# Three fp32r passes for the spatial unit's token tiles 1 to 3, with the slab split when a layer begins

## The reference, cut to what matters

```
for l in range(DEPTH):                                   # 2 layers
    h = rms_norm(x, norm_mix_g[l])                       # 512 x 1024
    parts = jnp.split(h @ w_in[l], split_points, axis=-1)
    q, k_c, v_c, k_s, v_s, k_w, v_w, nsa_g, sgu_in, s5_in, branch_g = parts
    y_a = nsa_attention(..., sigmoid(nsa_g), ...) @ w_attn_o[l]
    y_b = spatial_gating(sgu_in, ...) @ w_sgu_o[l]       # sgu_in: 512 columns
    y_c = s5_layer(s5_in, a_re, a_im, log_step, ...) @ w_s5_o[l]
    x = x + (g_a * y_a + g_b * y_b + g_c * y_c) @ w_mix_o[l]
    x = x + hierarchical_moe(rms_norm(x, norm_ffn_g[l]), ...)
```

## Time and profile before

| | |
|---|---|
| median of three runs | 1870.75 us |
| the profiled execution, its own time | 1874.76 us |
| its span | 1873.1 us |
| PE busy | 1833.1 us (98%) |
| DVE busy | 988.0 us (53%) |
| ACT busy | 488.3 us (26%) |
| POOL busy | 152.4 us (8%) |
| mean granted TensorE clock | 0.995 |

### The profile page before, as it was taken

The page is one execution under the profiler, slowest core; times in us unless marked ns, Lnnn a source line. Parts: engine busy times, 40 slices in busy tenths (PEclk is TensorE's granted clock), DMA queues, the critical chain, the costliest instruction groups (busy, mean ns, idle before and its releaser), DMA issues. The chain is left out here.

```text
span 1873.1 us, 26669 instructions
## 1 busy us (share of the span) xinstructions
PE 1833.1 (98%) x10352; PEld 1149.9 (61%) x10353; DVE 988.0 (53%) x1926; ACT 488.3 (26%) x881; POOL 152.4 (8%) x241
## 2 busy tenths in 40 slices
PE   7999999999999999999999999999999999999996
PEld 3887777788445455454457977778874545455443
DVE  6874555667334343342479565557663334343444
ACT  5423444433111111101154244443321111111112
POOL 4700000050000000000055000000400000000000
PEclk9999999999999999999999999999999999999998
DMA  5232111344999999999732311113369999999995
GB/s 173 70 125 69 68 68 46 113 143 196 404 426 427 425 426 426 422 428 425 328 110 71 124 68 68 46 58 123 121 272 427 427 427 425 428 422 427 421 427 213
DMA packets 61296, 482.92 MB, mean 258 GB/s; under 512 B 10256, under 2 KB 23056, under 8 KB 31504
## 3 DMA queue, kind: packets, MB, share of 16 engines
q1 hardware_dynamic: 61200, 481.59, 63.6%
HBM read 476.59 MB, written 4.19 MB: 257 GB/s over the span
## 5 line engine op out<-in xcount | busy, mean ns | idle before, releaser
L1979 DVE TENSOR_TENSOR x_tokens<-x_tokens,ps 128x512 f32<-128x512 f32 x240 | 160.6, 687 | 223.3 <-PE ps L1116 221.9
L1131 PE MATMUL ps<-arena,branch 128*64 128x512 f32 x512 | 230.3, 603 | 4.7 <-DMA slabs<-in_expert_w_down 4.7
L1131 PE MATMUL ps<-slabs,branch 128*64 128x512 f32 x512 | 230.4, 603 | 0.0
L1140 PE MATMUL ps<-arena 128*64 128x512 f32 x512 | 225.0, 592 | 0.0
L1141 PE MATMUL ps<-arena 128*64 128x512 f32 x512 | 225.0, 592 | 0.0
L1140 PE MATMUL ps<-slabs,arena 128*64 128x512 f32 x512 | 224.9, 592 | 0.0
L1141 PE MATMUL ps<-slabs,arena 128*64 128x512 f32 x512 | 224.9, 592 | 0.0
L853 PE MATMUL ps<-h_hi,w_parts 128*128 128x512 f32 x768 | 210.8, 408 | 1.5 <-DVE w_parts L1586 1.5
L1140 PEld LDWEIGHTS ps<-slabs,arena 128*64 128x64 f32 x512 | 70.1, 137 | 146.4 <-issue 146.4
L1140 PEld LDWEIGHTS ps<-arena 128*64 128x64 f32 x512 | 70.0, 137 | 145.5 <-issue 145.2
L853 PEld LDWEIGHTS ps<-h_hi,w_parts 128*128 128x128 f32 x768 | 135.1, 188 | 38.8 <-issue 9.2
(11 more groups left out here) (368 smaller groups left out, 3074.4 us busy)
## 6 DMA issues: line engine op xcount, KB each, us to landing
arena<-in_expert_w_gate SPq DMA_DIRECT2D x32, 2048.0 KB, 12.2
arena<-in_expert_w_up SPq DMA_DIRECT2D x32, 2048.0 KB, 16.7
arena<-in_expert_w_down SPq DMA_DIRECT2D x32, 2048.0 KB, 9.6
slabs<-in_expert_w_down SPq DMA_DIRECT2D x32, 2048.0 KB, 14.1
slabs<-in_expert_w_gate SPq DMA_DIRECT2D x30, 2048.0 KB, 15.1
slabs<-in_expert_w_up SPq DMA_DIRECT2D x30, 2048.0 KB, 19.6
slabs<-in_gate_w SPq DMA_DIRECT2D x24, 1024.0 KB, 4.8
slabs<-in_dense SPq DMA_DIRECT2D x22, 1024.0 KB, 5.8
```

Of the source, the lines that this page charges most:

```text
L1131: done = nc.tensor.matmul(ps[64 * b:64 * b + 64, BANK_Y[half], :], hidT[:, k, CAP * b:CAP * (b + 1)], w_down[b][:, k, half * 512:(half + 1 ...
L1140: nc.tensor.matmul(ps[0:64, BANK_GU[b], :], xk, low[:, k, :], start=(k == 0), stop=(k == ND - 1), tile_position=(0, 0))
L1979: v.tensor_tensor(xs, xs, ps[:, banks[n % len(banks)], :], ALU.add).then_inc(s["back_added"], 1)
```

## The change

The spatial unit's tile 0 stays plain fp32. Tiles 1 to 3 are multiplied in three passes of fp32r. For this, slab 0 is split when the layer begins: its high parts go into the third slab place (where slab 2 used to be loaded), its low parts into the place `x_lo`/`xn_tokens`. ACT makes the high parts in two copies of 128x2048, DVE subtracts blocks 0 to 3 and POOL blocks 4 to 7. All four `nsa_job`s stand ahead of the three new jobs. `h_hi` and `h_lo` are made earlier and in the order 1, 2, 3, 0. Slab 2 is loaded once all four tiles are done, and its high copy on ACT stands behind the last spatial evacuation and the small gates' copy. The counts of the semaphores shift by the new increments (`SGU_HI`, `SGU_LO`).

```diff
+        sgu_hi = w_parts[:, 2 * SLAB:3 * SLAB].rearrange("p (k c) -> p k c", k=ND)
+        sgu_lo = x_lo_place[:, 0:SLAB].rearrange("p (k c) -> p k c", k=ND)
...
-                    free = {3: (s["proj_done"], J_S5), 4: ...
+                    free = {2: (s["proj_done"], J_S5), 3: (s["proj_done"], J_S5), 4: ...
...
+                    def parts_job(n, t):                                     # PE
+                        out = bank_p(n)
+                        at = slice(t * P, (t + 1) * P)
+                        for part, (h, w) in enumerate(((h_hi, sgu_hi), (h_lo, sgu_hi), (h_hi, sgu_lo))):
+                            if part < 2:
+                                pe.wait_ge(s[("h_hi_ready", "h_lo_ready")[part]], t)
+                            for k in range(ND):
+                                if t == 1 and part == 0 and k % 4 == 0:
+                                    pe.wait_ge(s["w_hi_ready"], k // 4 + 1)
+                                if t == 1 and part == 2:
+                                    pe.wait_ge(*((s["w_lo_ready"], k + 1) if k < 4 else (s["w_lo_pool"], k - 3)))
+                                last = nc.tensor.matmul(out, h[:, k, at], w[:, k, :], start=..., stop=...)
+                        last.then_inc(s["proj_done"], 1)
...
+                    token_job(J_SGU, w_sgu, 0, S, 0)
+                    pe.wait_ge(s["small_in"], 16)
                     for t in range(NT):
-                        token_job(J_SGU + t, w_sgu, 0, S, t)  (and nsa_job(t) behind tiles 1 to 3)
+                        pe.wait_ge(s["hT_ready"], max(t, 1))
+                        nsa_job(t)
+                    for t in range(1, NT):
+                        parts_job(J_SGU + t, t)
...
+                    if layer == 0: (the two rotary Sin activations, moved to the front)     # ACT
+                    act.wait_ge(slab_in[0], 16)
+                    for half in range(2):
+                        ks = slice(4 * half, 4 * half + 4)
+                        nc.scalar.activation(sgu_hi[:, ks, :], view(slab[0], ND, S)[:, ks, :], ACT.Identity).then_inc(s["w_hi_ready"], 1)
                     act.wait_ge(s["small_in"], 16)
-                    act.wait_ge(s["bparam_in"], 16)
                     nc.scalar.activation(s5_small[0], small["lstep"], ACT.Exp).then_inc(s["step_ready"], 1)
+                    token_hi(1)
+                    token_hi(2)
                     (Exp of the magnitude, Sin and cosine of the angle)
+                    token_hi(3)
+                    token_hi(0)
                     for t in range(NT):
                         evac(J_SGU + t, ...)
+                        if t == 0:
+                            split_hi(1)
                     nc.scalar.activation(nsa_parts, ps[:, BANK_S[0], :], ACT.Identity).then_inc(s["nsa_parted"], 1)
+                    split_hi(2)
...
+                    dve.wait_ge(s["w_hi_ready"], 1)                          # DVE, behind hT
+                    for k in range(4):
+                        v.tensor_tensor(sgu_lo[:, k, :], view(slab[0], ND, S)[:, k, :], sgu_hi[:, k, :], ALU.subtract).then_inc(s["w_lo_ready"], 1)
                     (step, angle chain)
+                    for t in range(1, NT):
+                        low_tokens(t)
                     (polar chain)
                     low_tokens(0)
-                    low_tokens(1)
                     split_lo(LO_PIECES)
-                    low_tokens(2)
                     (two products of powers)
-                    low_tokens(3)
                     split_lo(LO_PIECES)
...
+                    pool.wait_ge(s["w_hi_ready"], 2)                         # POOL, ahead of all else
+                    for k in range(4, ND):
+                        g.tensor_tensor(sgu_lo[:, k, :], view(slab[0], ND, S)[:, k, :], sgu_hi[:, k, :], ALU.subtract).then_inc(s["w_lo_pool"], 1)
```

More of the change, by code:

```diff
@@ L95 @@
 LO_PIECES = 4
+SGU_HI, SGU_LO = 2, 4
 LO_COLS = SLAB // 2 // LO_PIECES
@@ L715, in token_job @@
                         last.then_inc(s["proj_done"], 1)
+                    def parts_job(n, t):
[9 more added lines that the diff above has]
+                                    pe.wait_ge(*((s["w_lo_ready"], k + 1) if k < 4 else (s["w_lo_pool"], k - 3)))
+                                last = nc.tensor.matmul(out, h[:, k, at], w[:, k, :], start=(part == 0 and k == 0), stop=(part == 2 and k == ND - 1))
+                        last.then_inc(s["proj_done"], 1)
                     def value_job(t):
@@ L962, in _ @@
                         if n % 4 == 0:
-                            pe.wait_ge(s["w_hi_ready"], m + 1)
+                            pe.wait_ge(s["w_hi_ready"], SGU_HI + m + 1)
                         if n == 0:
@@ L1258, in _ @@
                     nc.scalar.activation(cos1, sincos[3], ACT.Sin).then_inc(s["polar_ready"], 1)
-                    if layer == 0:
-                        nc.scalar.activation(rope_sin, rr, ACT.Sin, scale=rot_sign).then_inc(s["pro_act"], 1)
-                        nc.scalar.activation(rope_cos, r2, ACT.Sin).then_inc(s["pro_act"], 1)
+                    token_hi(3)
+                    token_hi(0)
                     def split_hi(k):
@@ L1512, in _, with low_tokens @@
                         ins.then_inc(s["hT_ready"], 1)
+                    def low_tokens(t):
+                        dve.wait_ge(s["h_hi_ready"], t if t >= 1 else NT)
+                        dve.wait_ge(s["nsa_done"], t + 1)
+                        cols = slice(t * P, (t + 1) * P)
+                        v.tensor_tensor(h_lo[:, :, cols], tile_of(t), h_hi[:, :, cols], ALU.subtract).then_inc(s["h_lo_ready"], 1)
+                    if layer == 0:
+                        dve.wait_ge(s["pro_act"], 2)
+                    dve.wait_ge(s["w_hi_ready"], 1)
+                    for k in range(4):
+                        v.tensor_tensor(sgu_lo[:, k, :], view(slab[0], ND, S)[:, k, :], sgu_hi[:, k, :], ALU.subtract).then_inc(s["w_lo_ready"], 1)
                     dve.wait_ge(s["small_in"], 16)
@@ L1566, in times @@
                         return v.tensor_tensor(to[:, 1].rearrange("p (a b) -> p a b", b=32), one[:, 1], two[:, 0], ALU.add)
-                    def low_tokens(t):
-                        dve.wait_ge(s["h_hi_ready"], t + 1)
-                        dve.wait_ge(s["proj_done"], J_SGU + t + 1)
-                        dve.wait_ge(s["nsa_done"], t + 1)
-                        cols = slice(t * P, (t + 1) * P)
-                        v.tensor_tensor(h_lo[:, :, cols], tile_of(t), h_hi[:, :, cols], ALU.subtract).then_inc(s["h_lo_ready"], 1)
                     lows = [0]
@@ L2112, in clear_told @@
                         pool.wait_ge(s["planes_clear"], cleared[0])
+                    if layer == 0:
+                        pool.wait_ge(s["pro_act"], 2)
+                    pool.wait_ge(s["w_hi_ready"], 2)
+                    for k in range(4, ND):
+                        g.tensor_tensor(sgu_lo[:, k, :], view(slab[0], ND, S)[:, k, :], sgu_hi[:, k, :], ALU.subtract).then_inc(s["w_lo_pool"], 1)
                     pool.wait_ge(s["small_in"], 16)
```

39 lines of the change are left out of this document (16 added, 23 removed).

## The result

The changed kernel takes 1893.74 us (median of 4 runs, 1891.81 to 1894.95), the kernel before 1870.49 beside it: ratio 1.0113, 95% interval [1.0096, 1.013]. Forecast were 1871.5 and a range of 1864 to 1876, so the prediction was wrong by 22 us. The profiled execution took 1891.81, its span 1890.1, against 1874.76 and 1873.1. What follows places the 17.0.

A forecast was written before the change was run, and what follows sets the result against it. PE's own work was taken to bound each layer's start. Gain 1.5 + 1.9 = 3.4 us, loss 4.2, so 0.8 slower: 1871.5 us against the median, range 1864 to 1876.

The forecast's parts named there:

- What the change saves on PE: Spatial tiles and small gates: three tiles at 5.57 instead of 6.95 us, gates 0.4 saved; ideal 4.5 us a layer.
- Rival (e): Spatial tiles 1 to 3: three passes cost 6.5 us each, not 5.57; 6.4 us slower, 1877.1; chance 0.04.
- The wait in front of tile 1: Second part of tile 1: PE waits for h_lo, 3.0 us in layer 0 and 2.6 in layer 1.
- rival (c): Tile 1's angle chain: the DVE/POOL port lock holds at every step; 3.2 us slower, 1874.0; chance 0.14.
- T4: Start of the first S5 job, ending the spatial stretch; forecast 1.5 us earlier in layer 0, 1.9 in layer 1.
- The later slab 2: Slab 2 issued at T4: waits at taps and first key job, 1.8 and 2.4 us, together 4.2 (2.2 to 7.6).
- the chain behind it: Behind slab 2's low parts: one times, variance, four times, 14.7 us, making c_pow ready at T4 + 25.2.
- Key job in layer 1: First key job, second part: two dear low pieces, 1.9 us of stall; 2.4 with the taps' 0.5.
- rival (d): First key job, both layers: all pieces beside POOL's 128x512 doublings, 7.6 us lost; 4.2 slower, 1875.0; chance 0.14.
- What I put at nothing: POOL's tables ending at 90.8 with at least 1 us slack before S5 output, and ACT's extra copies and order: no cost.

The follow-up runs named there:

- the late slab alone: The kernel before, with only slab 2 loaded after the four spatial jobs and its high copy later; no split of slab 0: 1885.46 against 1873.15 us.
- the padded kernels: The kernel before with 64 or 128 already met waits ahead of PE's first token transposes: start of layer 1 costs 0.15 to 0.17%, about 3 us.
- The experiment that holds the clock: The changed kernel with 16 discarded products ahead of the h_lo wait and 16 ahead of the taps, layer 0 only: 1888.26 us, ratio 1.0091.

## Why the prediction was wrong, by its own steps

- **What the change saves on PE: right.** Where nothing is waited for (tiles 2 and 3) a tile takes 5.44 (5.57 forecast), and the four small gates take 1.9 (2.0). Rival (e) is out.
- **The wait in front of tile 1: right place, upper end, and a term missing.** Layer 0: 3.0 taken of 0.8 to 4.4, 4.14 measured; the steps of 1.2 to 1.7 us, one for each block of POOL, show rival (c), the lock at every step of the angle chain, as the nearest. Behind the wait came 2.5 us of lowered clock, which no step had: T4 was 2.2 later, not 1.5 earlier. Layer 1: 2.6 taken, 1.6 measured, and that was luck. The low part was ready 14.1 behind the first job, where the forecast had 13.4 and its upper bound 14.4; the wait was short only because PE came 1.7 later, 1.5 of it by the clock in the first job. T4 was 1.45 earlier instead of 1.9. The Trainium skill, "SBUF — State Buffer", section "SBUF: two separate sides", states that of DVE and GpSimd the one that starts first holds the shared pair of ports for its whole instruction, and the other blocks. By that rule the low parts would come at the upper bounds: the 4.14 of layer 0 and the 14.1 of layer 1 agree.
- **The later slab 2: this is the step that failed.** Costed at 4.2 in all (2.2 to 7.6), it was worth 12 us alone and 16.8 in the changed kernel; in the profile, the way from T4 to the mixing grew by 7.3 and 7.9, so by 15.2. Of these, 9.2 are waits. The other 6.0 are slower products, which the prediction put at nothing. Slab and low parts were ready 10.8 (alone) and 11.8 and 11.1 (changed) behind T4, against 10.5: right to 1.3.
  In layer 0, and in both layers of the late slab alone, the term that was mis-sized is the chain behind it, "69.62 - 54.88 = 14.7", taken from a trace in which POOL's largest doublings began only after it. It ran into them: 19.2 and 18.4 alone, 17.5 in the changed kernel (64.34 to 81.84). By the prediction's own numbers the chain would have ended at 49.3 + 25.2 = 74.5, with the doublings from 79 on; measured, T4 was 3.2 later than the 49.3 and the doublings began at 76.00, 3 earlier. So the chain's length hung on an order of DVE and POOL that 3 us could turn, and I asked only what the key job's pieces would meet. The wait at the taps was then 4.7 (5.2 and 5.5 alone) instead of 0.5, and the clock fell behind it: from the taps to the mixing 2.7 more in layer 0.
- **Key job in layer 1: right place, too small a price.** There the chain took its 14.7 and the taps waited 1.2, but all of the job's pieces were dear, at 1.3 each, and not two of four. That is rival (d) in place: waits of 2.9 in the job and 1.2 at the taps, 4.1 in all, where 2.4 were forecast. The job and its neighbour needed 13.35 instead of 6.59, since beside the waits the clock was 0.85 and 0.81. The range left out that (c) and (d) come together, as they did.
- **What I put at nothing.** The tables ended at 86.5, no later than 90.8 allowed, and the S5 output waited for nothing: right. ACT's order was put in "0 to 0.2": behind the low part the bank of tile 2 is the next wait, 4.6 and 2.3, hidden in the changed kernel by the first.
- **The layer's start: not in the prediction.** 3.3 us of gap and 1.5 in a first job at a lowered clock, worth about 3 us of median by the padded kernels; the statement that even all bounds together make 6.6 left out both this and the clock.

Open is how the 16.8 of the slab divides between late start, clock and doublings in the changed kernel. The experiment that holds the clock lies 0.2% lower with overlapping intervals, and its way on shows that the three are not a sum.

## What to carry to other kernels

A duration read from the trace holds for the neighbours it had there: when a chain is shifted, lay the other engines' timelines beside its new place, piece by piece, before its old sum is used again, above all DVE beside POOL. In layer 0, waits of PE of 4.1 and 4.7 us were followed by 2.5 and 2.7 us more of slower products and small waits, so price the clock with the wait. And a load that was there long before it was needed is not free to be moved: the chain that hangs on it has to be followed to PE's next need and not only to its own use.

## What the runs showed of the hardware that was not expected

- PE's granted clock was 0.50 to 0.89 in the stretches of 4 to 10 us behind waits of 4.1 to 5.5 us (8 products in 3.78 instead of 1.98) and 0.85 and 0.81 over a key job with four waits of 0.2 to 1.3 each. It stayed at 1.00 behind a single wait of 1.6 (8 products in 2.11). The length of the wait alone does not tell: behind idle times of 1.90 the first job of layer 1 took 7.11 in the kernel before and 8.80 with the slab late alone. 16 products whose results are thrown away, in a wait of 4.1, kept it at 1.00.
- PE's idle time at the start of an unrolled layer changed from 1.9 to 4.4 and 5.3 us by 64 and 128 waits of no effect, 900 us ahead of it.
- Small DVE steps of 0.17 us took 1.21, 1.22 and 1.66 beside POOL's 128x512 fp32r subtractions, one step for each of POOL's instructions.
- Executions of the kernel before spread from 1867.4 to 1878.1 us. Each trace here, of whichever kernel, has two longer waits for expert weights, between 2.8 and 5.8 us together, so single spans of two kernels differ by a few us without any cause in the change. Even 12 runs against 29 left an interval 0.2% wide, 4 us.
